# Redistributing the mixer's convolution, cached key pages and pointwise product between GpSimd, VectorE, ScalarE and TensorE

## The reference

```python
def decoder_layer(x, pos0, pool_buf, conv_buf, past_k, past_v, mk, mv, p):
    x = x + 0.5 * swiglu_ffn(rms_norm(x, p['ln_ffn1']), p['w_ffn1_in'], p['w_ffn1_out'])
    y, new_pool, new_conv, k, v = mixer_groups(rms_norm(x, p['ln_mix']), pos0, pool_buf, conv_buf, past_k, past_v, p)
    x = x + y
    x = x + memory_attend(rms_norm(x, p['ln_cross']), mk, mv, p)
    x = x + 0.5 * swiglu_ffn(rms_norm(x, p['ln_ffn2']), p['w_ffn2_in'], p['w_ffn2_out'])
    return x, new_pool, new_conv, k, v
```

```python
    h = a * jax.nn.sigmoid(gate)
    ext = jnp.concatenate([buf, h], axis=1)
    y = lax.conv_general_dilated(ext, dw_w[:, None, :], window_strides=(1,), padding='VALID', ...) + dw_b
    y = jax.nn.silu(layer_norm(y, ln_g, ln_b))
    return y @ pw_w + pw_b, ext[:, -CONV_BUF:]
```

## Time and profile before

| | us |
|---|---|
| runs, median (lowest to highest) | 1488.61 (1487.62 to 1494.21) |
| the profiled execution | 1488.8 |
| its span | 1487.0 |
| busy in the span: PE | 1416.9 |
| DVE | 947.4 |
| ACT | 597.1 |
| POOL | 124.3 |

### The profile page before, as it was taken

The page is one execution under the profiler, slowest core; times in us unless marked ns, Lnnn a source line. Parts: engine busy times, 40 slices in busy tenths (PEclk is TensorE's granted clock), DMA queues, the critical chain, the costliest instruction groups (busy, mean ns, idle before and its releaser), DMA issues. The chain is left out here.

```text
span 1487.0 us, 28022 instructions
## 1 busy us (share of the span) xinstructions
PE 1416.9 (95%) x10902; PEld 1339.5 (90%) x10902; DVE 947.4 (64%) x1359; ACT 597.1 (40%) x854; POOL 124.3 (8%) x167
## 2 busy tenths in 40 slices
PE   5999999979999999999999999998799999999998
PEld 5999999858967799999999999998598778999998
DVE  5666656986655566665466664589766465666643
ACT  4333434444543343333343333442554433433332
POOL 3000000252010110000000000005310100000000
PEclk8999999999999999999999999999899999999999
DMA  8666445437467676654456654544465766556552
GB/s 260 170 169 169 157 159 166 157 130 252 151 231 251 236 184 169 169 168 157 139 163 166 169 169 157 174 152 142 140 236 170 247 242 219 150 163 168 162 172 94
DMA packets 298890, 263.95 MB, mean 178 GB/s; under 512 B 7287, under 2 KB 268917, under 8 KB 298775
## 3 DMA queue, kind: packets, MB, share of 16 engines
q1 hardware_dynamic: 279058, 203.28, 45.4%
q0 software_dynamic: 13776, 48.97, 9.3%
q10 hardware_dynamic: 5972, 10.54, 2.2%
HBM read 254.80 MB, written 8.56 MB: 177 GB/s over the span
## 5 line engine op out<-in xcount | busy, mean ns | idle before, releaser
L959 DVE TENSOR_TENSOR w_lo<-raw_weights,w_hi 128x1024 fp32r<-128x1024 f32 (+2 forms) x404 | 451.0, 1159 | 139.5 <-ACT w_hi L710 138.1
L1459 PE MATMUL pairs<-h_hi,w_hi 128*128 128x288 f32 x1760 | 522.9, 297 | 15.1 <-DVE h_lo L962 6.4
L1459 PE MATMUL pairs<-h_lo,w_hi 128*128 128x288 f32 x1760 | 523.7, 298 | 0.0
L1459 PE MATMUL pairs<-h_hi,w_lo 128*128 128x288 f32 x1760 | 521.5, 296 | 0.0
L710 ACT ACTIVATE w_hi<-raw_weights 128x1024 fp32r<-128x1024 f32 (+2 forms) x404 | 383.3, 999 | 280.6 <-PE pairs L1459 243.3
L1459 PEld LDWEIGHTS pairs<-h_hi,w_hi 128*128 128x128 f32 x1760 | 334.1, 190 | 19.1 <-issue 10.3
L1459 PEld LDWEIGHTS pairs<-h_lo,w_hi 128*128 128x128 f32 x1760 | 333.7, 190 | 0.6
L1459 PEld LDWEIGHTS pairs<-h_hi,w_lo 128*128 128x128 f32 x1760 | 333.3, 189 | 0.0
L1459 PE MATMUL pairs<-g_lo,w_hi 128*128 128x288 f32 x704 | 208.2, 296 | 0.0
L1459 PE MATMUL pairs<-g_hi,w_hi 128*128 128x288 f32 x704 | 208.1, 296 | 0.0
L1459 PE MATMUL pairs<-g_hi,w_lo 128*128 128x288 f32 x704 | 207.0, 294 | 0.0
(11 more groups left out here) (277 smaller groups left out, 1515.1 us busy)
## 6 DMA issues: line engine op xcount, KB each, us to landing
raw_weights<-in_w_ffn_in SPq DMA_DIRECT2D x176, 512.0 KB
raw_weights<-in_w_ffn_out SPq DMA_DIRECT2D x32, 1024.0 KB
raw_weights<-in_w_in SPq DMA_DIRECT2D x18, 1024.0 KB
mem_kv<-in_cache_mem_k POOLq DMA_DIRECT2D x16, 1024.0 KB, 5.4
raw_weights<-in_w_ckv SPq DMA_DIRECT2D x16, 1024.0 KB
raw_weights<-in_w_ffn_out SPq DMA_DIRECT2D x16, 768.0 KB
raw_weights<-in_w_out SPq DMA_DIRECT2D x8, 1024.0 KB
...
```

Source lines behind the costliest of these rows:

```text
L959: return dve.tensor_tensor(out, in0, in1, op)
L1459: return pe.matmul(out, lhsT, rhs, start=start, stop=stop, **kw)
```

## The change

- **GpSimd.** The samples' cached rows are convolved first, as soon as they are turned (`states_taken`), with zeros in the four places of the new rows; then eight of the prompt's taps (`POOL_TAP` = 23 to 30), into `conv_part`: per tap two products and, but for the first, two sums; then the pooling; then value pages 2, 3, 6, 7 when the last `w_in` unit is done, and 4 and 5 after the last score.
- **VectorE.** The new rows' share of the samples' convolution is eight small instructions (`new_taps`) after `pool_in`. Taps 0 to 14 stay where they are. Tap 15 moves behind the second value scaling, whose wait for the first key copy now stands ahead of it; 16 to 22 move behind the probabilities' bias. VectorE copies the transposed keys of samples 4 and 5 (`key_rows`), and adds `conv_part`. The split of the first `w_out` unit comes after the samples' queries are spread. The layer norm's centring moves behind the sample scores' bias.
- **Places.** Ten places for cached pages. Keys 0 to 3 each have one of their own; `att_k2` lies on the second half of `y`, where the rotation's scratch is, so keys 2 and 3 wait for `z_done`.
- **ScalarE.** Issues key pages 2 and 3 after `z_done`, before it copies key 0; copies keys 0 to 3, makes all eight exponentials, copies keys 6 and 7.
- **TensorE.** All key transposes come before `att_pt`; the last two score matmuls stand behind the two halves of `att_pt`; the layer norm's sums come after two of the tokens' transposes; all value pages come before `pw`; the first `w_out` unit takes its rows in the order 0, 1, 4, 5, 6, 7, 2, 3.

The core of the diff:

```diff
+POOL_TAP = 23
@@ POOL
-                pool.wait_ge(pool_in, L + 1)
+                pool.wait_ge(states_taken, L + 1)
                 pool.sem_inc(pool_passed, 1)
-                for c in range(2):
-                    pooling(c)
-                pool.sem_inc(pooled, 1)
-
                 for c in range(2):
                     windows = ap(cxt, c * CX + CBUF + SEQ, [[CBUF + NEW, SAMPLES], [1, NEW], [1, CONV_K]])
...
                 pool.sem_inc(conv_new_done, 1)
+                pool.wait_ge(fresh_ready, L + 1)
+                for j in range(POOL_TAP, CONV_K):
+                    w = PROWS["conv_dw_w"][0] + 2 * j
+                    for c in range(2):
+                        out = conv_part[:, c, :] if j == POOL_TAP else (win_b, win_c)[c][:, 0:SEQ]
+                        pool.tensor_scalar(out, cxt[:, c, j:j + SEQ], prm_all[:, L, w + c:w + c + 1], None, ALU.mult)
+                    pool.drain()
+                    if j > POOL_TAP:
+                        for c in range(2):
+                            pool.tensor_tensor(conv_part[:, c, :], conv_part[:, c, :], (win_b, win_c)[c][:, 0:SEQ], ALU.add)
+                        pool.drain()
+                pool.sem_inc(part_done, 1)
+                pool.wait_ge(pool_in, L + 1)
+                for c in range(2):
+                    pooling(c)
+                pool.sem_inc(pooled, 1)
@@ ACT
                     if n == 8:
-                        for b in range(6):
+                        act.wait_ge(pages_landed, 16)
+                        for b in (2, 3):
+                            numbers = page_numbers(act, b)
+                            act.wait_ge(z_done, L * 2 + 1)
+                            act.sem_inc(act_passed, 1)
+                            load_pages(act, L, b, numbers)
+                        for b in range(4):
                             att_keys(b)
-                            if b in (2, 3):
-                                prompt_exp(2 * b - 4)
-                                prompt_exp(2 * b - 3)
+                        for hd in range(HEADS):
+                            prompt_exp(hd)
+                        for b in range(6, SAMPLES):
+                            att_keys(b)
@@ DVE
+                def new_taps():
+                    for lag in range(NEW):
+                        w = PROWS["conv_dw_w"][0] + 2 * (CONV_K - 1 - lag)
+                        for c in range(2):
+                            out = conv_acc[:, c, SEQ:T].rearrange("p (b t) -> p b t", b=SAMPLES)[:, :, lag:]
+                            src = fresh[:, 2 + c, :].rearrange("p (b t) -> p b t", b=SAMPLES)[:, :, 0:NEW - lag]
+                            stt(out, src, prm_all[:, L, w + c:w + c + 1], out, ALU.mult, ALU.add)
+                        dve.drain()
...
+                def key_rows(b):
+                    t = TURNS["att_k"][b]
+                    dve.wait_ge(score_done, L * (2 * SAMPLES) + b - 1)
+                    pair = acc(L, t)
+                    dve.tensor_copy(att_kt[:, b % 2, :, :].rearrange("p h c -> p (h c)"), pair.rearrange("p e c -> p (e c)")).then_inc(kt_dve, 1)
+                    dve.drain()
...
-                taps(26, CONV_K)
-                dve.sem_inc(conv_done, 1)
+                taps(20, POOL_TAP)
+                dve.wait_ge(part_done, L + 1)
+                tt(conv_acc[:, :, 0:SEQ], conv_acc[:, :, 0:SEQ], conv_part[:, :, :], ALU.add).then_inc(conv_done, 1)
@@ PE
-                    unit(L, 0, UNITS["wout"] + n, pair, y, wait=mixed if n == 0 else None)
+                    unit(L, 0, UNITS["wout"] + n, pair, y, wait=mixed if n == 0 else None, order=(0, 1, 4, 5, 6, 7, 2, 3) if n == 0 else None)
```

168 lines of the change are left out of this document (91 added, 77 removed).

## The result

The changed kernel took 1498.32 us (median of 11 runs, 1495.81 to 1504.37), the kernel before, run beside it, 1488.61 (median of 11, 1484.04 to 1494.21). The ratio is 1.0079, with a 95% interval of 1.0066 to 1.0092: **slower by 0.8%**, more than the 0.5% that a measurement of this kernel can tell from no change. The profiled execution has a span of 1495.1 us (before 1487.0).

What follows compares the result with a forecast made beforehand. VectorE and TensorE were nearly full in the `w_in` units, VectorE causing most of TensorE's idle time. Front +12.5, layers -3.2 and -8.0 gave +1.3; clock +1.7 made +3.0 on 1488.8: 1492 us, range 1477 to 1505.

Steps and rivals of the forecast that it cites:

- the likeliest case: Whole kernel: the same time as before within what a measurement can tell, 1483 to 1496 us, chance 0.42.
- term 1: Front: the samples' convolution, moved forward on GpSimd, delays VectorE's splits by 2.5 us in layer 0, 0.9 in layer 1.
- term 2: `w_in` units: GpSimd's eight taps slow VectorE; `pool_in` comes 6.6 us late in layer 0, 5.9 in layer 1, +12.5 us.
- Term 3: From `pool_in` to the key transposes behind the scores: ScalarE's longer queue against shorter waits, -0.9 and -3.3 us.
- Term 4: Key pages: keys 4 to 7 have early places and need no wait; 14.4 us, -4.8 and -7.2 by layer.
- Term 5: Tail: later samples' scores and centring against the pointwise product moved last, together +2.5 us per layer.
- Clock: `w_in` units: new idle is followed by one stretch of 3.5 us of matmuls at 1.2 GHz, +1.7 us.
- (a): Front: the shared ports cost little, only 3 to 5 us of the 12.5 are left; 1481 us or less, chance 0.28.
- (b): Front: GpSimd's one-input instructions hold VectorE too, 0.55 us more for each of 14; +13.9, 1505 us, chance 0.16.
- (c): Mixers: each new idle stretch is followed by 3 us at 1.2 GHz; +7.3, 1499 us, chance 0.11.
- (d): Tail: GpSimd's taps arrive late, `part_done` after 330 us; 1500 us or more, chance 0.03.

Runs made afterwards that it cites:

- key 0 first: Changed kernel, but ScalarE copies key 0 before it waits for the rotation and issues pages 2 and 3: 1491.62 us, ratio 1.0029 to the kernel before.

## Why the prediction was right or wrong

The forecast was 1492 us, the time 1498.3: inside the range of 1477 to 1505, outside the likeliest case's own 1483 to 1496, and on the side to which I gave 0.30 (slower by over 0.5%), not on the likeliest, no change. The range holds the time only because I had widened it for the rivals, and the terms below missed in both directions, so that it lies no further off is in part luck. By the five terms, the forecast +3.0 us, the mixers' timelines +11.9:

- **Terms 1 and 2, the front.** `z_done` was to come 6.6 - 1.4 = 5.2 us late in layer 0 and 5.9 - 2.5 = 3.4 in layer 1; it came 5.6 and 6.8 late, 3.8 us more in sum. Two slips stand in my sum: the 0.5 us that VectorE waits for ScalarE are taken off twice, once inside the 4.6 and once beside it (once only, `pool_in` comes 7.1 and 6.4 late), and layer 1's delay by the samples' convolution is 0.9 in term 1 and 1.8 in term 2. The mechanism and its main price held: 35 us of taps (34), a sum at 0.3 (0.36 to 0.39), a scaling at 0.15 (0.09); the taps cost 4.8 and 5.5 us, where 4.6 were forecast. Two small sizes were off. The samples' convolution was to delay the gated columns by 2.5 us in layer 0, which it did, but by 0.9 in layer 1, where it was 4.0 (three splits grew there, by 2.2, 1.3 and 4.1 us); taken away it gave 0 and 2.3 us. And `new_taps` took 4.15 and 3.61 us instead of 1.6 to 2.3.
- **Term 3, from the rotation to the transposes behind the scores: the step that failed.** I had 7.4 + 4.0 + 1.2 = 12.6 us. The 1.2 held to 0.03. The scores began 9.7 and 8.8 us behind the rotation: my sum ended with the end of key 0's copy, while the release for VectorE and TensorE stands behind the issue of page 4 and a drain (copy ended at 313.63, TensorE went on at 314.21), and the copy itself began 0.6 us later than by my sum. Then TensorE had its transposes, 1.97 us at the lower clock in layer 0, where I took 1.09. The scores took 5.5 us, not 4.0. Together 6.6 us. As a change against before, this part of the term was forecast as +0.5 and -0.8 and came as +4.2 and +2.5, a miss of 7.0. The two differ because of a slip in layer 1: 12.6 us against the 12.9 of before are -0.3, not -0.8; the scores' growth from 2.9 us is counted short. The run with key 0 first shows that this hung on one order in ScalarE's program: start and scores together fell by 4.5 and 3.7 us, the time by 7.4 us. I had priced that queue instruction by instruction as +2.0 us and then let it be eaten by other gains; I should have asked which of its steps needed `z_done` at all.
- **Term 4, the keys.** -4.8 and -7.2 forecast, -3.2 and -6.5 measured: 16.0 and 15.1 us, not 14.4. (1.1 us of each is the column sum, which moved to the tail.) The waits for pages are gone as forecast; TensorE still waits 1.85 us for the normalised probabilities, and in layer 0 another 1.52 for a copy.
- **Term 5, the tail.** +2.5 per layer forecast, +1.2 measured, the column sum included. The samples' softmax is late as I said (2.03 us of wait), and the later place of the pointwise product is worth 3 us, not the 1.4 I gave it: 1.9 of wait, and 1.4 of lower clock, which the same wait did not bring in the kernel before.
- **Clock.** 1.7 us were set aside. The eighth units alone show more: by their mean clock, 4.55 x (1 - 0.62) + 4.13 x (1 - 0.66) = 3.1 us, and the scores and transposes of key 1 took 0.95 + 2.6 us longer than before for the scores and about 0.9 in layer 0 for the transposes. That is 7 to 8 us in all, most of it already counted in the terms above.

The sum of the misses: 3.8 + 7.0 + 2.3 - 2.6 - 1.7 = 8.8, and 3.0 + 8.8 = 11.8.

Of the **rivals**, (a) falls: the ports cost what was forecast, 10 us. (b), one-input instructions that hold VectorE for nearly their whole length, falls too: 0.09 us each, not 0.7. That was the rule of the Trainium skill, "SBUF — State Buffer", section "Who interferes with whom", that whoever comes first has the shared ports for the whole instruction (the page says this of VectorE's two-port modes; of a VectorE instruction with two SBUF inputs it says that it contends with a GpSimd instruction that reads SBUF); for GpSimd's two-input sums it is nearer to the runs (0.36 to 0.39 of 0.73 us lost), for its one-input scalings they don't bear it out. (c) is what came, beside the misread queue: idle stretches of 4 us, each followed by some 3 us or more at 1.2 GHz (estimated from the mean clocks above), and a time of 1499 us. The nearness of the number is luck in part: of its three idle stretches per layer, the one before the third unit did not grow in layer 0 (1.05 us, as before) and only to 1.83 in layer 1, and the queue's share was not in it. I gave it 0.11, because I added idle stretches one by one as if each were short; term 2 and term 3 each made one of 4 us. (d) didn't happen: no wait for GpSimd's part stands in the trace.
